# A one-layer hybrid decoder step: where the triangular inverse is masked and copied, where the convolution taps run, and the order of the input projection's columns

## The reference, cut to what matters

```
a_h, a_b, a_c = jnp.split(pa, 3, axis=-1)                    # group A, tiles 0..5
a_conv, new_conv_a = causal_dwconv(a_c * a_h, conv_a, W['a_conv_w'][l])
y_a = a_b * a_conv
b_val, b_gate = jnp.split(pb, 2, axis=-1)                    # group B, tiles 6..9
b_conv, new_conv_b = causal_dwconv(b_val * jax.nn.sigmoid(b_gate), conv_b, W['b_conv_w'][l])
y_b = jax.nn.silu(layernorm(b_conv + W['b_conv_b'][l], W['b_ln_g'][l], W['b_ln_b'][l], B_LN_EPS))
# group C, tiles 10..16: the RWKV-7 delta rule, per token
sa = jnp.einsum('bhij,bhj->bhi', S, -kk_t)
S = (S * w_t[:, :, None, :] + sa[..., None] * (kk_t * a_t)[:, :, None, :]
     + v_t[..., None] * k_t[:, :, None, :])
# group D, tiles 17, 18: trailing means over 2/4/8/16 tokens minus the token
```

## Time and profile before

| | us |
|---|---|
| median of 3 runs | 1296.12 |
| lowest, highest | 1294.04, 1298.65 |
| span of the profiled execution | 1293.3 |
| PE busy in it | 1201.6 (93%) |
| DVE busy | 635.5 (49%) |
| ACT busy | 324.1 (25%) |
| POOL busy | 91.0 (7%) |
| mean granted clock of TensorE | 0.947 |

### The profile page before, as it was taken

How to read it: one execution, slowest core, us unless ns; L and a number is a source line. 1 busy time by engine, 2 the same in 40 slices (tenths; PEclk the granted TensorE clock), 3 DMA queues, 4 the chain that set the end, 5 groups by cost and what they waited for, 6 DMA issues and landing times. The chain is left out here.

```text
span 1293.3 us, 22199 instructions
## 1 busy us (share of the span) xinstructions
PE 1201.6 (93%) x9206; PEld 1158.4 (90%) x9206; DVE 635.5 (49%) x944; ACT 324.1 (25%) x480; POOL 91.0 (7%) x94
## 2 busy tenths in 40 slices
PE   6999999999999699898789899969999999999993
PEld 6999999999998699897667768959999999999993
DVE  4443334333344858949876622465433334333445
ACT  5321121211213434122222211224121122112121
POOL 0000000000000400202311300040000000000002
PEclk9999999999999699998999867969999999999997
DMA  6322232222223022191010000303222223223211
GB/s 224 99 98 77 86 98 66 96 83 86 92 66 97 17 66 84 54 96 28 1 33 2 1 1 1 100 17 99 67 96 84 88 89 97 82 81 99 74 56 69
DMA packets 34365, 92.11 MB, mean 71 GB/s; under 512 B 10496, under 2 KB 10880, under 8 KB 34176
## 3 DMA queue, kind: packets, MB, share of 16 engines
q1 hardware_dynamic: 32576, 87.26, 23.5%
q10 hardware_dynamic: 1728, 3.99, 0.8%
HBM read 87.95 MB, written 3.28 MB: 71 GB/s over the span
## 5 line engine op out<-in xcount | busy, mean ns | idle before, releaser
L290 PE MATMUL ps<-xh,wh 128*128 128x272 f32 x1840 | 544.4, 296 | 37.0 <-DVE xl L382 31.1
L292 PE MATMUL ps<-xh,wl 128*128 128x272 f32 x1840 | 538.8, 293 | 0.0
L291 PE MATMUL ps<-xl,wh 128*128 128x272 f32 x1840 | 536.2, 291 | 0.0
L290 PEld LDWEIGHTS ps<-xh,wh 128*128 128x128 f32 x1840 | 352.7, 192 | 43.1 <-issue 18.3
L291 PEld LDWEIGHTS ps<-xl,wh 128*128 128x128 f32 x1840 | 353.8, 192 | 0.2
L292 PEld LDWEIGHTS ps<-xh,wl 128*128 128x128 f32 x1840 | 352.8, 192 | 0.0
L269 ACT ACTIVATE wh<-raw 128x1024 fp32r<-128x1024 f32 (+1 forms) x163 | 167.7, 1033 | 353.3 <-PE ps L292 266.5
L274 DVE TENSOR_TENSOR wl<-raw,wh 128x1024 fp32r<-128x1024 f32 (+1 forms) x163 | 190.9, 1193 | 51.8 <-ACT wh L269 51.6
L292 PE MATMUL ps<-hh,wl 128*128 128x272 f32 x704 | 202.8, 288 | 0.0
L290 PE MATMUL ps<-hh,wh 128*128 128x272 f32 x704 | 202.7, 288 | 0.0
L291 PE MATMUL ps<-hl,wh 128*128 128x272 f32 x704 | 202.1, 287 | 0.0
(11 more groups left out here) (281 smaller groups left out, 942.3 us busy)
## 6 DMA issues: line engine op xcount, KB each, us to landing
raw<-in_w_gu SPq DMA_DIRECT2D x88, 512.0 KB, 3.7
raw<-in_w_d SPq DMA_DIRECT2D x32, 512.0 KB, 3.5
raw<-in_w_in SPq DMA_DIRECT2D x19, 512.0 KB, 3.6
raw<-in_w_d SPq DMA_DIRECT2D x16, 384.0 KB, 3.1
raw<-in_w_out SPq DMA_DIRECT2D x8, 512.0 KB, 3.7
x<-in_x ACTq DMA_DIRECT2D x8, 272.0 KB, 6.6
out_y<-x SPq DMA_DIRECT2D x8, 272.0 KB, 2.1
con<-in_con ACTq DMA_DIRECT2D x1, 1062.5 KB, 9.1
```

The costliest lines, as they stand in the source:

```text
L290: pe.matmul(out[:, n], wh[:, s, j], right_h[:, j, col], start=opens and j == order[0], stop=False)
L291: pe.matmul(out[:, n], wh[:, s, j], right_l[:, j, col], start=False, stop=False)
L292: last = pe.matmul(out[:, n], wl[:, s, j], right_h[:, j, col], start=False, stop=closes and j == order[-1])
```

## The change

Three things change, all in the mixer.

1. **Masks and copies of the inverse.** POOL's 48 mask products and the buffer's use in the levels are gone. DVE adds the identity to N once per block and pair (two ops of 128 x 256), makes the first inverse by a mask from it (two more), and PE transposes it. In a level PE multiplies the whole N + 1 with T; DVE applies the level's mask, which now holds the diagonal too, when it takes the product out of PSUM (128 x 256); so `xx` holds 1 + X, the product of stage 3 + 2l is the new T in full, and ACT copies it out (128 x 512). The sample recurrence's masks move from POOL to DVE (step q2).
2. **Taps.** Both halves of a tap stay on DVE, as a pair with semaphores of their own. `fill` is called seven times per block, and every third call does two taps.
3. **Column order.** `IN_TILES` is now C, D (n = 7, 8), b_val, b_gate (9 to 12), a_c (13, 14), a_h (15, 16), a_b (17, 18). What hangs on a tile moves with it; what hangs on m stays. SP's list of DMAs is the same, row for row.

```
-LORA, K0, K1, R0, R1, V0, V1, AC0, AC1, DD0, DD1, AH0, AH1, AB0, AB1, BV0, BV1, BG0, BG1 = range(19)
-IN_TILES = (16, 12, 13, 10, 11, 14, 15, 4, 5, 17, 18, 0, 1, 2, 3, 6, 7, 8, 9)
+LORA, K0, K1, R0, R1, V0, V1, DD0, DD1, BV0, BV1, BG0, BG1, AC0, AC1, AH0, AH1, AB0, AB1 = range(19)
+IN_TILES = (16, 12, 13, 10, 11, 14, 15, 17, 18, 6, 7, 8, 9, 4, 5, 0, 1, 2, 3)
...
-        c[:, CCOL["lev"] + n * P:][:, :P] = (s // (2 * b) == t // (2 * b)) & (s // b != t // b) & (s < t)
+        near = (s // (2 * b) == t // (2 * b)) & (s // b != t // b)
+        c[:, CCOL["lev"] + n * P:][:, :P] = near & (s < t if n == 0 else s > t) | (s == t)
...
@@ wkv_pe
-                pe.wait_ge(S("lev"), t * 12 + p + 1)
+                pe.wait_ge(S("tt1"), 2 * t + p + 1)
                 for h in range(2):
-                    last = pe.matmul(b[:, P * h:P * h + P], nlv[:, 0, p, h], ident, start=True, stop=True)
+                    last = pe.transpose(b[:, P * h:P * h + P], tt_[:, p, 1, h], ident)
...
-                    pe.wait_ge(S("lev"), t * 12 + 2 * l + p + 1)
                     pe.wait_ge(S(f"r{1 + 2 * l}"), 2 * t + p + 1)
                     for h in range(2):
-                        last = pe.matmul(b[:, P * h:P * h + P], nlv[:, l % 2, p, h], tt_[:, p, 0, h], start=True, stop=True)
+                        last = pe.matmul(b[:, P * h:P * h + P], nrb[:, p, h, 0], tt_[:, p, 0, h], start=True, stop=True)
...
@@ wkv_act
+            for p in range(2):
+                b = done(3, p)
+                act.activation(tt_[:, p, 0], b[:, 0:2 * P].rearrange("p (h c) -> p h c", h=2), ACT.Copy).then_inc(S("r3"), 1)
...
-                    s = 2 + 2 * l
+                    s = 3 + 2 * l
                     b = done(s, p)
-                    act.activation(xx[:, p], b[:, 0:2 * P].rearrange("p (h c) -> p h c", h=2), ACT.Copy).then_inc(S(f"r{s}"), 1)
+                    k = 0 if l < 5 else 1
+                    act.activation(tt_[:, p, k:2].rearrange("p k h c -> p (k h c)"), b[:, 256 * k:512], ACT.Copy).then_inc(S(f"r{s}"), 1)
...
@@ wkv_dve
+                dve.tensor_tensor(nrb[:, p, :, 0], nrb[:, p, :, 0], idb, ADD).then_inc(S("unit"), 1)
...
+                dve.tensor_tensor(tt_[:, p, 1], nrb[:, p, :, 0], C_("lev").unsqueeze(1).to_broadcast([P, 2, P]), MUL
+                                  ).then_inc(S("tt1"), 1)
...
-                    s = 3 + 2 * l
+                    s = 2 + 2 * l
                     b = done(s, p)
-                    dve.tensor_tensor(both, b[:, 256 * k:512], both, ADD).then_inc(S(f"r{s}"), 1)
+                    dve.tensor_tensor(xx[:, p], b[:, 0:2 * P].rearrange("p (h c) -> p h c", h=2),
+                                      C_("lev", k=l * P).unsqueeze(1).to_broadcast([P, 2, P]), MUL).then_inc(S(f"r{s}"), 1)
                 fill()
...
@@ mixer_pe
-            in_out(pe, BG1)
+            in_out(pe, NIN - 1)
...
@@ fill
-                k0, fills = taps, fills + 1
-                taps = min(CONVB, taps + 1 + (fills % 6 == 0))
-                conv(k0, taps)
+                fills += 1
+                for _ in range(2 if fills % 3 == 0 else 1):
```

More of the change, by code:

```diff
@@ L104, in constants @@
     s, t = s[:32], t[:, :32]
+    for n in range(2):
+        c[:32, CCOL["slev"] + 32 * n:][:, :32] = (s // (2 << n) == t // (2 << n)) & (s >> n != t >> n) & (s < t)
     c[:32, CCOL["smask"]:][:, :32] = (s // NT == t // NT) & (s < t)
@@ L653, in mixer_sp, with tap @@
             sp.dma_start(o["o_ss"], s1t[:]).then_inc(S("out"), 16)
+        def tap(eng, k, p):
+            w = par[:, PCOL["bw"] + 2 * k + p:PCOL["bw"] + 2 * k + p + 1]
+            z1 = zb[:, p, k:k + NP_]
+            z2 = zb[:, p, 542:].rearrange("p (b c) -> p b c", c=34)[:, :, k:k + NT]
+            y1, y2 = yb[:, p, 0:NP_], comp(yb[:, p, DT])
+            if k == 0:
+                eng.tensor_scalar(y1, z1, w, par_("bb", p), MUL, ADD)
+                return eng.tensor_scalar(y2, z2, w, par_("bb", p), MUL, ADD)
+            eng.scalar_tensor_tensor(y1, z1, w, y1, MUL, ADD)
+            return eng.scalar_tensor_tensor(y2, z2, w, y2, MUL, ADD)
         def mixer_pool(pool):
@@ L690, in mixer_pool @@
             pool.tensor_tensor(d2[64:P, 1, 15:], d1[64:P, 1, 15:], d1[64:P, 1, 7:-8], ADD).then_inc(S("pool_d"), 1)
[L692 to L709, removed]
         NSTAGE = 20
@@ L1059, in q_pe @@
                 pe.wait_ge(S("q7"), 2)
-                pe.wait_ge(S("conv"), 1)
+                pe.wait_ge(S("taps0"), CONVB)
+                pe.wait_ge(S("taps1"), CONVB)
                 for p in range(2):
@@ L1133, in q_dve @@
                     last.then_inc(S(step), 1)
+                if step == "q2":
+                    dve.wait_ge(S("q2"), p + 1)
+                    for k in range(2):
+                        last = dve.tensor_tensor(qnlv[0:NS, k, p], qnrb[0:NS, p, :, 0],
+                                                 C_("slev", NS, k * NS, NS).unsqueeze(1).to_broadcast([NS, 2, NS]), MUL)
+                    last.then_inc(S("q_lev"), 1)
                 if step == "q3":
@@ L1558, in fill @@
                 nonlocal taps, fills
-                k0, fills = taps, fills + 1
-                taps = min(CONVB, taps + 1 + (fills % 6 == 0))
-                conv(k0, taps)
+                fills += 1
+                for _ in range(2 if fills % 3 == 0 else 1):
+                    if taps < CONVB:
+                        for p in range(2):
+                            if taps == 0:
+                                dve.wait_ge(S("glu"), p + 1)
+                            else:
+                                dve.wait_ge(S(f"taps{p}"), taps)
+                            tap(dve, taps, p).then_inc(S(f"taps{p}"), 1)
+                        taps += 1
             def beside(t, s):
```

49 lines of the change are left out of this document (12 added, 37 removed).

## The result

| | before | after |
|---|---|---|
| median of 16 runs each, us | 1298.64 | 1309.49 |
| lowest, highest | 1293.66, 1315.98 | 1306.44, 1318.78 |
| profiled execution: own time | not recorded | 1312.12 |
| its span | 1293.3 | 1310.3 |

The ratio of after to before is 1.0077, 95% interval 1.0049 to 1.0105: slower by about 10 us, where I had said slower by about 5 and a range up to 1308, so the median lies 1.5 us outside.

What follows compares the result with a forecast made beforehand. It took PE, busy 93% of the 1293.3 us span, as the bound, with DVE bounding a recurrence level. Terms +7.7 - 5.4 - 2.0 - 1.1 + 2 + 3.5 = +4.7 us gave a median of about 1301, range 1290 to 1308.

Steps and rivals of the forecast that it cites:

- Part 1: Start of the recurrence: input gaps go, but state stores delay the first output weight; PE begins at 587.6, +7.7 us.
- Rival A: At the start, stores don't hold the load, weight lands some 4 us after issue; 1285 us, chance 0.08.
- Part 2: Stage 3 of each block: shorter wait for the first inverse, -1.35 us each, -5.4 for four.
- Parts 3 and 4: Levels 1 to 5 -2.0 us, block 1's states' wait -1.1; clock +2 in first levels, +3.5 in block 0's start.
- Bare and double levels: A level without a second tap takes 3.08 us against 3.84; a second tap makes it 4.4.
- part 4: Clock at 1.2 GHz: +2 us over four blocks' first levels, +3.5 in stages 0 to 2 of block 0.
- DVE's early turn: In the levels, whatever follows DVE's turn delays the next level; block 3's levels +1.2 us, all blocks together -2.0.
- Part 5: Nothing elsewhere: no time added for the 31st tap, POOL's share moved to DVE or block 2's sample masks.
- Rival C: DVE's side steps lengthen levels, block 0 stays at 1.2 GHz, start at 590; +13, 1309 us, chance 0.12.
- Rival B: Start late but recurrence gains in full, clock back within stage 1; -3.5 or 0, 1294 us, chance 0.33.

Runs made afterwards that it cites:

- experiment 3: The changed kernel with SP issuing the first two output weights' loads ahead of the o_a and o_d state stores: 1300.51 us, ratio to before 0.9994.
- experiment 1: The changed kernel with the old column order, its masks, copies and taps kept as changed: 1303.58 us, ratio to before 1.0019.
- experiment 4: The changed kernel with DVE's share of b_root moved behind level 5's masks in block 3: 1308.77 us, ratio to before 1.0074.
- experiment 9: The changed kernel with four unread constant matmuls on PE in level 5's gap of block 3: 1311.38 us, ratio to before 1.01.
- experiment 6: The changed kernel with the four o_d stores issued before input tile 16's load, and two output-weight loads before the o_a stores: 1292.29 us.
- experiment 11: The changed kernel with the x side steps' twelve 512-column matmuls on 128 rows, 32 to 127 zero on one side: 1289.26 us, ratio to before 0.9915.
- experiment 12: The kernel before with the x side steps' twelve 512-column matmuls on 128 zero-padded rows, nothing else: 1284.83 us, ratio 0.9898.
- experiment 10: The changed kernel with o_d stores and output loads early, DVE side steps later, and x-step matmuls on 128 zero-padded rows: 1266.33 us, ratio to before 0.9750.
- experiment 5: The kernel before profiled once more, nothing changed: one run, 1313.79 us, span 1312.0.
- experiment 2: The kernel before with the new column order alone, masks still on POOL: 1319.91 us, ratio 1.0091.

## Why the prediction was right and wrong

*Part 1, the start: right.* +7.7 forecast, +7.51 measured; each step of the chain came within half a microsecond (571.4, 560.1, 581.2, 587.6 forecast, 571.8, 560.05, 581.05, 587.42 read). The gaps of 0.97 and 3.38 us are gone. Choosing the whole 21.1 us from first store to split, and not the load's own 12.9, was right: it took 21.0, and the load alone 16.8, not 12.9. The Trainium skill (DMA: Bandwidth & Descriptors, Queues, rings and completion order) has a queue's descriptors consumed in ring order on each DMA engine. The trace agrees with its 21.0, and experiment 3 does from the other side: a load ahead of the stores doesn't wait for them. Rival A is out.

*Part 2, stage 3: right, a little small.* -1.35 per block forecast, -1.89 measured in blocks 1 to 3. In block 0, -1.09 when it kept its clock (experiment 1, 7.32 against 8.41).

*Parts 3 and 4, levels and the cold start: right for block 0, near for block 1, too small in block 3.* Stages 0 to 3 of block 0: forecast -1.35 + 3.5 = +2.15, measured +2.25. Bare and double levels: 3.08 and 4.4 forecast, 3.25 and 4.48 measured; but the three terms named for the double level (2.35, 0.72, 1.65) add up to 4.72, so the 4.4 was nearer than its working. The sums of the levels, with the +2 of part 4 shared out evenly, were to be -1.9, +0.3, -0.1, +1.7; they were -1.88, +1.80, -0.81, +5.48. Block 1's excess, 1.5 in the levels and 1.75 in the tail (forecast at -1.1, +0.65 here), is for the most part the clock of one execution. Experiments 1, 4 and 9, with the same block 1, take 35.3 to 35.4 for levels and tail together, 0.7 to 0.8 less than before's 36.1, where -0.8 was forecast; experiments 3, 6 and 11 take 37.0 to 37.3, after 38.55. After's clock is at 0.50 from 656 to 662 us, in the tail; that of experiment 4 stays at 1.00 there. Block 3's +5.48 is the term of DVE's early turn, mis-sized, and something else besides. I counted b_root as one step among others, and it is 3.5 us on DVE that PE releases just as level 5 begins; but 2.6 of the 5.48 are x0 at 1.2 GHz, which belongs to the next part. Without it the block's levels are at +2.9, against +1.7. Experiments 11 and 12 put the block at +4.0, again with 2.2 of x0's clock in it.

*Part 5, "nothing elsewhere": the step that failed.* It put block 3's x steps and tail at no change; the tail took 42.35 us in the profile, 33.5 of them at a granted 0.50. I had looked at the clock only behind idle gaps. The clock stays down there because of the matmuls with few rows (experiments 10 to 12), and the moment of the fall moves between executions of one and the same kernel (experiment 5), so that one profile of before, a short one, understated what before takes and made its tail look given. Of the 17.0 us between the profiles 7.6 are the tail and 2.6 are x0: 10.2 us of clock that no term of the sum holds. Against the sum's 4.7 the profiles are 12.3 too far apart: tail +7.6, block 3's levels +3.8 (x0's 2.6 in it), block 1's levels and tail +3.2 (the clock of one execution), stages 0 to 3 -1.5, block 2 -0.7, start -0.2. With full rows the medians are 4.4 apart, and block 1's levels, +1.8 in the first pair of profiles, are +0.1. That the 4.4 is so close to the forecast's 4.7 is in part luck, since its terms err both ways.

*Rival C* named the time that came, 1309, by another sum: a start at 590 and a block 0 at 1.2 GHz throughout (+5) did not come, its longer levels did in block 3, and the tail isn't in it. *Rival B*, the clock back within stage 1, is out: block 0 had 0.52 for 14.5 us.

*Still open:* how much of the 10.9 us between the medians is the tail. In before about a third of the runs are long. All eight profiles with the new recurrence and 32 rows have the long tail, and of three with the old one (before twice, experiment 2) two have it; what the other runs had in theirs isn't recorded. I have not shown by a run whether the longer level 5 makes it so; experiment 9 took the gap out and did not bring the short tail back, so the gap alone does not. Why one execution of before falls to 1.2 GHz from 658 to 685 us and another doesn't is open too.

The Trainium skill (TensorE: Matmul & The Clock Gate, Why this matters for your kernels) tells one to avoid idle gaps of PE between bursts. By that alone the stretch of x0 and the tail, with PE busy 55.13 of 55.50 us, should have been at 2.4 GHz; it was at 1.2, and experiments 9 and 10 decide for the measurement: filling the gap did nothing for the tail, using the rows took 20.8 us off it.

## What to carry to other kernels

Look at the granted clock of every stretch where the engine is *busy*, not only behind gaps, and be suspicious of long stretches at half clock made of matmuls with few rows: padding them with zero rows added no column of PE's work here and gave 20 to 22 us in the two changed kernels. A store made of many small runs belongs where nothing waits behind it in its queue: ask of each reordering which stores it pushes against which load. And profile the kernel before twice when its runs fall into bunches, before any stretch of it is taken as given.

## What the runs showed of the hardware

- The eight state stores, 4.3 us to issue, took 19.2 us to land (experiment 3, 559.82 to 579.02), and in after the load behind them took 16.8 where an input weight takes 3.6. Four alone had landed 12.4 us after their first issue (experiment 6); the other four, moved earlier in the same queue, cost no time that can be seen.
- Matmuls of 512 columns kept TensorE at 1.2 GHz with 32 rows in use, with the small matmuls among them 55 us long, PE being busy all the time. With 128 rows, 96 of them zero on one side, it was at 2.4 GHz again before the second x step (experiment 10). Without any such matmul, among matmuls of 64 columns, it fell to 1.2 GHz as well in one of two executions of before (experiment 5, from 658 us). That zeros serve was not to be expected from any row of the trace.
- The tap of 512 columns on DVE takes at most 0.75 us in after, with POOL silent, against up to 1.26 beside POOL's masks in before.
